# A two-block transformer step: the attention output product in two halves, and the output written before a branch

## The reference

```python
mod = jnp.einsum('bd,de->be', jax.nn.silu(c), w_ada[l]) + b_ada[l]
sh1, sc1, g1, sh2, sc2, g2 = [m[:, None, :] for m in jnp.split(mod, 6, axis=-1)]
h = _rms(x, norm1_g[l]) * (1.0 + sc1) + sh1
c_q, c_kv, k_pe, dq, dk, dv = jnp.split(h @ w_in[l], IN_SPLITS, axis=-1)
o_mla = _mla(c_q, c_kv, k_pe, ...)       # 8 heads x 64; q from w_uq, k and v from w_ukv
o_diff = _diff_attn(dq, dk, dv, ...)     # 4 heads x 128, each head's output under _rms
x = x + g1 * (jnp.concatenate([o_mla, o_diff], axis=-1) @ w_o[l])
h2 = _rms(x, norm2_g[l]) * (1.0 + sc2) + sh2
x = x + g2 * _hmoe(h2, ...)              # 2 of 16 experts per token, D_EXPERT = 512
```

## Time and profile before

| | us |
|---|---|
| median of 3 runs | 2050.57 (2049.27 to 2053.07) |
| profiled execution | 2052.58 |
| its span, first to last instruction | 2050.7 |
| PE busy | 1840.4 (90%) |
| DVE, ACT, POOL busy | 620.0, 486.7, 351.6 |
| mean granted TensorE clock | 0.936 |

### The profile page before, as it was taken

How to read it: one execution, slowest core, us unless ns; L and a number is a source line. 1 busy time by engine, 2 the same in 40 slices (tenths; PEclk the granted TensorE clock), 3 DMA queues, 4 the chain that set the end, 5 groups by cost and what they waited for, 6 DMA issues and landing times.

```text
span 2050.7 us, 29034 instructions
## 1 busy us (share of the span) xinstructions
PE 1840.4 (90%) x12173; PEld 1078.1 (53%) x12173; DVE 620.0 (30%) x1265; ACT 486.7 (24%) x830; POOL 351.6 (17%) x306
## 2 busy tenths in 40 slices
PE   8999999989957699999999999999995896599996
PEld 7977999757935333323332333233322786454442
DVE  6777554346444500100000000010004585501102
ACT  5844443324402110001000010000002553321120
POOL 3000000000000399999920000000001000000000
PEclk9998999988978699999999999999997988789998
DMA  6446664446522899999999999999995440569994
GB/s 191 152 137 205 207 206 172 159 154 207 185 82 82 300 408 404 417 415 411 409 409 417 411 411 404 419 410 411 402 421 157 129 144 1 205 266 419 420 419 199
DMA packets 185008, 583.04 MB, mean 284 GB/s; under 512 B 11162, under 2 KB 77355, under 8 KB 158241
## 3 DMA queue, kind: packets, MB, share of 16 engines
q1 hardware_dynamic: 182256, 575.09, 73.1%
q0 software_dynamic: 2608, 5.97, 1.1%
HBM read 579.96 MB, written 1.05 MB: 283 GB/s over the span
## 4 chain that ended last, share of the span: by engine, by line
PE 70%; DMA 13%; DVE 9%; ACT 4%; issue 2%; SPq 2%; DVEq 0%; ACTq 0%
PE ps L1702 16%; PE ps L440 9%; PE ps L441 8%; PE ps L442 8%; DMA ring<-in_moe_w_out 8%; PE ps L2137 6%; PE ps L1707 5%; PE ps L1738 4%; DMA ring<-in_moe_w_in 3%; PE ps L2161 3%; SPq L1550 1%; DVE wlo L473 1%; PE ps L1743 1%; PE ps L575 1%; PE ps L2122 1%
## 5 line engine op out<-in xcount | busy, mean ns | idle before, releaser
L1702 PE MATMUL ps<-ring,xg 128*64 128x512 f32 x1624 | 411.7, 602 | 13.1 <-ACT sgm L1812 5.8
L473 DVE TENSOR_TENSOR wlo<-raw,whi 128x2048 fp32r<-128x2048 f32 (+6 forms) x97 | 213.8, 2208 | 227.8 <-ACT whi L465 227.5
L1702 PEld LDWEIGHTS ps<-ring,xg 128*64 128x64 f32 x1624 | 121.8, 137 | 220.0 <-issue 208.6
L465 ACT ACTIVATE whi<-raw 128x2048 fp32r<-128x2048 f32 (+6 forms) x97 | 178.7, 1845 | 230.5 <-PE ps L442 89.3
L440 PE MATMUL ps<-xh,whi 128*128 128x272 f32 (+1 forms) x712 | 212.7, 299 | 4.1 <-DVE xl L540 3.8
L1738 PE MATMUL ps<-ring,ahm 128*64 128x512 f32 x824 | 204.5, 597 | 11.7 <-DMA ring<-in_moe_w_out 10.9
L442 PE MATMUL ps<-xh,wlo 128*128 128x272 f32 (+1 forms) x712 | 210.0, 295 | 0.0
L441 PE MATMUL ps<-xl,whi 128*128 128x272 f32 (+1 forms) x712 | 209.7, 295 | 0.0
L2070 POOL TENSOR_SCALAR lnt<-lnt,h 128x384 f32<-128x384 f32 x120 | 188.6, 1572 | 12.2
L1876 DVE TENSOR_TENSOR sgm<-sgm,ps 128x512 f32<-128x512 f32 x28 | 18.2, 685 | 512.2 <-PE ps L1707 512.2
L704 POOL DMA_DIRECT2D lnt<-in_ln_gain x4 | 2.2, 560 | 858.1 <-issue 525.6
(11 more groups left out here) (567 smaller groups left out, 2471.4 us busy)
## 6 DMA issues: line engine op xcount, KB each, us to landing
ring<-in_moe_w_in SPq DMA_DIRECT2D x203, 1024.0 KB, 17.9
ring<-in_moe_w_out SPq DMA_DIRECT2D x103, 1024.0 KB, 19.9
ring<-in_w_gate SPq DMA_DIRECT2D x29, 1024.0 KB, 13.2
raw<-in_ffn_w_in SPq DMA_DIRECT2D x28, 1024.0 KB
ring<-in_w_down SPq DMA_DIRECT2D x26, 1024.0 KB, 12.6
raw<-in_w_ada SPq DMA_DIRECT2D x24, 1024.0 KB
more<-in_moe_w_in SPq DMA_DIRECT2D x21, 1024.0 KB, 18.1
ring<-in_w_up SPq DMA_DIRECT2D x20, 1024.0 KB, 11.5
```

The costliest lines, as they stand in the source:

```text
L465: e.activation(whi[0:rows, s % NSPL, 0:n], raw[0:rows, i % NRAW, 0:n], ACT.Copy).then_inc(S.hi.s, S.hi.up((s,)))
L473: e.tensor_tensor(wlo[0:rows, s % NSPL, 0:n], raw[0:rows, i % NRAW, 0:n], whi[0:rows, s % NSPL, 0:n].bitcast(F32), ALU.subtract).then_inc( ...
L1702: e.matmul(ps_[b][64 * v:64 * v + 64, :], a[:, kk_, 64 * v:64 * v + 64], both[v][:, k, 512 * b:512 * b + 512], start=kk_ == 0, stop=kk_ == 7)
```

## The change

- Start: ScalarE's split of w_in's first chunk goes behind the two squares.
- `dve_neighbours_end` goes from behind the angles to right behind the cq turn.
- VectorE's low part of w_in's last chunk goes ahead of the k products.
- x6 is cut in two. Its first four column blocks (the MLA heads) are turned between `values 2` and `probs 3`; `wo` chunks 0 and 1 are multiplied right behind `values 3`, under the norm of the differential heads. The last four (x6b) follow when `od` is ready, then chunks 2 and 3, first all of group 0, then all of group 1 (`pe_last_two`, which is used with XTILES elsewhere).
- Gate, sum, mean square and root are done group by group; ScalarE scales both groups; the transposes of group 0 for x7 (the first four) come ahead of group 1's.
- The end: VectorE multiplies by g2 out of PSUM and adds to h within the first round; SyncE writes the output ahead of its branch. Where the further rounds run, they add to h and write it again.

The diff, cut to what the text speaks of (signal names, the labels and the unchanged half of the first norm are left out):

```diff
@@ -620,7 +620,7 @@
             bank.give((key, 2), (dve, key, "sum", 2))
-        for t, n, cc in XTILES:
+        for t, n, cc in tiles:
             for m in range(4):
@@ -2286,13 +2286,10 @@
             for q in range(2):
-                o = w["y"][:, t, 512 * q:512 * q + 512]
-                p = bk(key, "Y", t, q)[:, :]
-                if r == 0:
-                    ins = e.tensor_copy(o, p)
-                else:
-                    ins = e.tensor_tensor(o, o, p, ALU.add)
-                ins.then_inc(C.dve.s, C.dve.up((key, "out")))
+                a = slice(512 * q, 512 * q + 512)
+                e.tensor_tensor(w["y"][:, t, a], bk(key, "Y", t, q)[:, :], g2t[:, a], ALU.mult).then_inc(C.dve.s, C.dve.up((key, "out")))
+            e.wait_ge(C.dve.s, C.dve.n)
+            e.tensor_tensor(h[:, t, :], h[:, t, :], w["y"][:, t, :], ALU.add).then_inc(C.dve.s, C.dve.up((key, "result", t)))
@@ -2302,6 +2299,7 @@
                 load_ring(e, C, SLOTS, False)
+                sp_out_again(e)
             for r, key in enumerate(ROUNDS2):
@@ -2312,6 +2310,8 @@
                         e.wait_ge(C.dve.s, C.dve.n)
+                    else:
+                        e.wait_ge(landed["out"].s, landed["out"].at("all"))
                     dve_pairs(e, C, key, w2, r + 1)
@@ -2356,22 +2356,45 @@
-    def act_mean_sq(e, key, full):
+    def act_mean_sq(e, s):
         for t in range(2):
-            e.wait_ge(dve.s, dve.at(full, t))
+            e.wait_ge(dve.s, dve.at("ln3", t))
             e.activation(hn[:, t, :], h[:, t, :], ACT.Square, scale=1.0 / 32, accum_out=rs[:, 0, t:t + 1]).then_inc(
-                act.s, act.up((key, "sum")))
-        if key == "rms2":
-            act_spread(e, "g2", g2t)
-        e.wait_ge(dve.s, dve.at(key, "root"))
-        e.activation(hn[:, 0, :], h[:, 0, :], ACT.Copy, scale=rs[:, 1, 0:1]).then_inc(act.s, act.up((key, "hn")))
-    def dve_mean_sq(e, key):
-        e.wait_ge(act.s, act.at(key, "sum"))
+                act.s, act.up(("rms1", "sum")))
+        split_hi(e, M, s)
+        e.wait_ge(dve.s, dve.at("rms1", "root"))
+        e.activation(hn[:, 0, :], h[:, 0, :], ACT.Copy, scale=rs[:, 1, 0:1]).then_inc(act.s, act.up(("rms1", "hn")))
...
+    def act_gated_norm(e):
+        for t in range(2):
+            e.wait_ge(dve.s, dve.at("x1", t))
+            e.activation(hn[:, t, :], h[:, t, :], ACT.Square, scale=1.0 / 32, accum_out=rs[:, 0, t:t + 1]).then_inc(
+                act.s, act.up(("rms2", "sum", t)))
+            if t:
+                act_spread(e, "g2", g2t)
+            e.wait_ge(dve.s, dve.at("rms2", "root", t))
+            e.activation(hn[:, t, :], h[:, t, :], ACT.Copy, scale=rs[:, 1, t:t + 1]).then_inc(act.s, act.up(("rms2", "hn", t)))
+    def dve_gated_norm(e):
+        e.wait_ge(act.s, act.at("spread", "g1", 1))
+        for t in range(2):
+            e.wait_ge(pe.s, pe.at("wo", "tile", t))
+            for q in range(2):
+                a = slice(512 * q, 512 * q + 512)
+                e.tensor_tensor(pj[:, t, a], bank("wo", t, q)[:, :], g1t[:, a], ALU.mult).then_inc(dve.s, dve.up(("wo", "sum", t)))
+            e.wait_ge(dve.s, dve.n)
+            e.tensor_tensor(h[:, t, :], h[:, t, :], pj[:, t, 0:1024], ALU.add).then_inc(dve.s, dve.up(("x1", t)))
+            e.wait_ge(act.s, act.at("rms2", "sum", t))
+            e.tensor_scalar(rs[:, 0, t:t + 1], rs[:, 0, t:t + 1], RMS_EPS, None, ALU.add).then_inc(dve.s, dve.up())
+            dve_rsqrt(e, rs[:, 1, t:t + 1], rs[:, 0, t:t + 1], rtmp[:, t:t + 1], ("rms2", "root", t))
@@ -2612,12 +2635,12 @@
         pe_values(e, 2)
+        e.wait_ge(dve.s, dve.at("o1"))
+        pe_turn(e, "x6", src_n, QTILES, 4)
         pe_probs(e, 3)
         pe_values(e, 3)
-        e.wait_ge(dve.s, dve.at("od"))
-        pe_turn(e, "x6", src_n, QTILES, 8)
         acc = {(t, q): bank.take(e, "wo", t, q) for t, _, _ in QTILES for q in range(2)}
-        for j in range(4):
+        for j in range(2):
             wh, wl = (w.rearrange("p (i n) -> p i n", i=2) for w in weights(e, M, ("wo", j)))
@@ -2625,14 +2648,30 @@
                         ins = mm3(e, acc[t, q][:, :], xh[:, k, cc:cc + n], xl[:, k, cc:cc + n],
-                                  wh[:, i, 512 * q:512 * q + 512], wl[:, i, 512 * q:512 * q + 512], k == 0, k == 7)
-            ins.then_inc(pe.s, pe.up(("wo", j), used(M, ("wo", j))))
-        for t, q in acc:
-            bank.give(("wo", t, q), (dve, "gated", t, q))
+                                  wh[:, i, 512 * q:512 * q + 512], wl[:, i, 512 * q:512 * q + 512], k == 0, False)
+            ins.then_inc(pe.s, pe.up(used(M, ("wo", j))))
+        e.wait_ge(dve.s, dve.at("od"))
+        pe_turn(e, "x6b", lambda t, k: src_n(t, 4 + k), QTILES, 4)
+        e.wait_ge(dve.s, dve.at("x6b", "lo", 3))
+        pe_last_two(e, "wo", acc, None, [("wo", 2), ("wo", 3)],
+                    lambda m, cc, n: (xh[:, 4 + m, cc:cc + n], xl[:, 4 + m, cc:cc + n]), [], QTILES)
         pe_spread(e, "g2", pool)
-        e.wait_ge(act.s, act.at("rms2", "hn"))
-        e.wait_ge(dve.s, dve.at("rms2", "hn"))
-        pe_turn(e, "x7", src_n, QTILES, 8)
+        p = {}
+        def turn(k, t):
+            if t == 0:
+                p[k] = bank.take(e, "x7", k)
+            return e.transpose(p[k][:, 128 * t:128 * t + 128], src_n(t, k), idn)
+        e.wait_ge(act.s, act.at("rms2", "hn", 0))
+        for k in range(4):
+            turn(k, 0)
+        e.wait_ge(act.s, act.at("rms2", "hn", 1))
+        for k in range(8):
+            if k >= 4:
+                turn(k, 0)
+            turn(k, 1).then_inc(pe.s, pe.up(("x7", "T", k)))
+            bank.give(("x7", k), (dve, "x7", "lo", k))
         pe.label(("end_mid",))
@@ -2641,8 +2680,7 @@
         act_spread(e, "g1", g1t)
-        split_hi(e, M, s)
-        act_mean_sq(e, "rms1", "ln3")
+        act_mean_sq(e, s)
         split_hi(e, M, s + 1)
@@ -2707,14 +2745,14 @@
         act_probs(e, 2)
+        act_turn(e, "x6", QTILES, 4, xh)
         act_probs(e, 3)
         e.wait_ge(dve.s, dve.at("o2"))
         e.activation(od2, od, ACT.Square).then_inc(act.s, act.up(("osq",)))
-        act_turn(e, "x6", QTILES, 8, xh, gain_o)
-        for j in range(4):
-            split_hi(e, M, s)
-            s += 1
-        act_mean_sq(e, "rms2", "x1")
+        split_hi(e, M, s)
+        s += 1
+        act_turn(e, "x6b", QTILES, 4, xh[:, 4:8], gain_o)
+        act_gated_norm(e)
         act_turn(e, "x7", QTILES, 8, xh, gain_x3, shift_x3, tmpT)
@@ -2825,13 +2863,13 @@
         dve_turn(e, "cq", QTILES, 5, cq[:, 0], cq[:, 1], gain_cq)
+        dve_neighbours_end(e)
         split_lo(e, M, s)
         s += 1
         e.wait_ge(act.s, act.at("lat"))
         e.tensor_scalar(rs[:, 0, 0:4], r4[:, :], RMS_EPS, None, ALU.add).then_inc(dve.s, dve.up())
         dve_rsqrt(e, r4[:, :], rs[:, 0, 0:4], rtmp[:, 0:4], ("r4",))
         dve_angles(e)
-        dve_neighbours_end(e)
         for j in range(3):
@@ -2853,15 +2891,16 @@
         dve_head_rms(e, "ksq", 96, 64, pe2[:, :], rk16)
+        split_lo(e, M, s)
+        s += 1
         e.wait_ge(dve.s, dve.n)
         e.tensor_tensor(k5[:, :, :, 0:64], k5[:, :, :, 0:64], rk16[:, :, :].unsqueeze(3).to_broadcast([128, 2, 8, 64]), ALU.mult).then_inc(
             dve.s, dve.up())
         for t in range(2):
             e.tensor_tensor(k4[t][:, :, 64:96], kpe[:, t, :].unsqueeze(1).to_broadcast([128, 8, 32]),
                             rk16[:, t, :].unsqueeze(2).to_broadcast([128, 8, 32]), ALU.mult).then_inc(dve.s, dve.up(("kk",)))
-        for _ in range(2):
-            split_lo(e, M, s)
-            s += 1
+        split_lo(e, M, s)
+        s += 1
         for i in range(2):
@@ -2885,8 +2924,10 @@
         dve_values(e, 1)
+        dve.label(("o1",))
         dve_probs(e, 2)
         dve_values(e, 2)
+        dve_turn(e, "x6", QTILES, 4, xh, xl)
         dve_probs(e, 3)
@@ -2899,25 +2940,15 @@
         e.tensor_tensor(od, od, r1.unsqueeze(3).to_broadcast([128, 2, 4, 128]), ALU.mult).then_inc(dve.s, dve.up(("od",)))
-        dve_turn(e, "x6", QTILES, 8, xh, xl, gain_o)
-        for j in range(4):
-            split_lo(e, M, s)
-            s += 1
-        e.wait_ge(pe.s, pe.at("wo", 3))
-        e.wait_ge(act.s, act.at("spread", "g1", 1))
-        for t in range(2):
-            for q in range(2):
-                a = slice(512 * q, 512 * q + 512)
-                e.tensor_tensor(pj[:, t, a], bank("wo", t, q)[:, :], g1t[:, a], ALU.mult).then_inc(dve.s, dve.up(("gated", t, q)))
-                e.wait_ge(dve.s, dve.n)
-                e.tensor_tensor(h[:, t, a], h[:, t, a], pj[:, t, a], ALU.add).then_inc(dve.s, dve.up(("x1", t)))
-        dve_mean_sq(e, "rms2")
+        split_lo(e, M, s)
+        s += 1
+        dve_turn(e, "x6b", QTILES, 4, xh[:, 4:8], xl[:, 4:8], gain_o)
+        dve_gated_norm(e)
         dve_turn(e, "x7", QTILES, 8, xh, xl, gain_x3, shift_x3, tmpT)
         dve.label(("end_mid",))
         return s
-    y2 = w2["y"]
```

(33 more changed lines are left out.)

4 lines of the change are left out of this document (2 added, 2 removed).

## The result

The changed kernel is faster. In a first timing its median was 2024.9 us against 2049.9 us (ratio 0.9872, 95% interval 0.9843 to 0.9900), in a second, on another occasion, 2029.0 against 2051.3 (0.9887, 0.9867 to 0.9906). That is 26 and 23 us, where the forecast had 22.2. The first median lies inside the range, 0.9 us above its low end of 2024; the ratio times the median of before, 2049.9, gives 2023.7, just under it. The times alone do not refute 22.2, which lies inside both intervals (20.5 to 32.2 us and 19.3 to 27.3). The profiles, cut into stages, do: the four gains are there nearly as forecast, and the gain as a whole is about 4 us larger.

The account below looks back on a forecast made before the run. TensorE was taken to bound the expert pairs, with the attention part a serial stretch whose waits also lower the clock. A 2.8 + B 5.8 + C 10.4 + D 3.2 = 22.2 us off 2050.6: 2028.4, range 2024 to 2038.

Parts of the forecast that it names:

- A: Start of the stage: squares ahead of w_in's first split, sums ready sooner; gain 2.8 us (1.5 to 2.9).
- B: w_uq to first scores: no vp wait, ukv sooner, w_in's last chunk at full clock; gain 5.8 us (4.3 to 7.5).
- x6 in front: Between the heads: x6's first transposes, copies and subtractions ahead of values 3 cost 1.7 us.
- C: Output product: first half under the differential heads' norm, end by groups; gain 10.4 us (8 to 10.8), net of 1.7.
- D: Kernel's end: g2 multiplied out of PSUM, output DMA ahead of SyncE's branch; gain 3.2 us (2.4 to 5).
- Rival 1: Clock falls once more, ahead of values 3 or w_in's last chunk: costs 1.7 in C, 1.5 in B; 2031.6 us; 24%.
- Rivals 2 and 5: 2: A and B end at something unmoved, 2037 us; 5: w_o's first half not under the norm, 2036; together 15%.
- The prediction's row: Head transposes: clock rose to 1.00 at 1679.5 and stayed to 1686.9, read as transposes keeping it up.
- whatever the attention part saves arrives at the end as it is: Expert pairs: eight rounds of 28.2 us at clock 1.00 stay unchanged, if the weights keep pace.
- rival 3: Expert pairs: gains ahead of them are given back, DMA share being 1.01; D alone remains, 2047 us; 5%.

Follow-up runs that it names:

- only_wo: Kernel before with only x6 in two halves, half of w_o's product during the heads' norm and the end by token groups: ratio 0.9932.
- wo_output: Kernel before with the w_o halves, the end by token groups and the output ahead of SyncE's branch, without the first two gains: ratio 0.9925.
- fill: Changed kernel with 36 and 10 unused matmuls in TensorE's waits for the router's masks and for sel: ratio 0.9870.

## Why the prediction was right and where it fell short

Means over the profiles with and without each part, in us:

| stage | without | with | gain | forecast |
|---|---|---|---|---|
| gc to scores 0 (A, B) | 105.6 (7 profiles) | 97.0 (8) | 8.6 | 8.6 |
| scores 0 to norm (x6 in front) | 46.0 (7) | 46.8 (9) | -0.8 | -1.7 |
| norm to sel (C) | 64.7 (7) | 52.2 (10) | 12.5 | 12.1 |
| sel to last sg | 217.9 (7) | 217.0 (4) | 0.9 | 0 |
| last sg to y | 25.5 (5) | 23.4 (4) | 2.1 | 0 |
| y to end (D) | 14.7 (8) | 11.8 (9) | 2.9 | 3.2 |
| sum | | | 26.2 | 22.2 |

- **A was right**: 2.8 alone.
- **B was right in its parts**, within 0.5: the 4 us ahead of w_ukv, the fallen clock there, the shrunken wait and the last chunk at full clock. Rival 1's clock fall ahead of the last chunk did not come in any profile. Behind the chunk lies a wait that the prediction doesn't name, the 1.8 us for `qk`, and in five of the nine profiles with B the clock fell there.
- **C was right**: 12.5 for 12.1. For the 1.7 us of x6 between the heads I have 0.8 out of two groups that each spread over 4 to 6 us; this size stays open. The wait ahead of values 3 was 2.5 us for the forecast's 3.0, and the clock stayed up in all profiles of the changed kernel. In `only_wo` and `wo_output` the same 2.5 us wait was followed at once by 3.4 us at 0.50, into the w_o product. So rival 1's fall in C was near, and its way of telling safe waits from others, by their length alone (2.3 against 2.9 us), is not borne out. Rivals 2 and 5 are out.
- The Trainium skill, TensorE: Matmul & The Clock Gate, "Part 4: PE-mode transpose", has transposes not counting as busy. x6's eight don't decide on it: they took 1.0 us, from 1701.0, when the clock rose behind 3.4 us of products. The prediction's row does not either as it was read, since 5.2 of its 7.4 us are score products. But the same trace of before disagrees with the page, in two places. At the stage's start TensorE sat idle and then ran x5's 16 transposes and nothing else; at the head transposes it had run w_in's last chunk. Windows over the idle time, x5 up to the rise, and what follows; then over the chunk, the first 4 us of head transposes, and the last of them:

```profile
1571.50:1584.30 12.80, 0.00 (x0) 0.50 1.03 294
1584.40:1587.20 2.80, 2.80 (x13) 0.50 0.02 7
1587.40:1594.00 6.60, 3.94 (x22) 1.00 0.49 156
...
1666.10:1675.20 9.10, 9.10 (x45) 0.50 0.62 230
1675.30:1679.30 4.00, 4.00 (x20) 0.50 0.54 156
1679.50:1680.80 1.30, 1.30 (x14) 1.00 0.65 271
```

  The clock rose behind 2.9 us of x5's transposes, with 12.9 us of idle ahead of them. At the heads 9 us of 128x160 products left it low, and it rose 4.1 us into the transposes.
- **D was right**: 2.9 for 3.2, the branch 3.6 for 3.4. Alone it gave 2.2: y to the end took 12.5 us, 0.8 more than in the changed kernel, with VectorE's four steps as long as there; the 0.8 lies between the last sum and the end, and its cause is open.
- **The step that failed is "whatever the attention part saves arrives at the end as it is"**, with the pairs entered as zero: 3.0 us came there. The earlier trace rows shows one round in the middle, at 1.00, and I read all eight from it. Five of the seven distances from one `sg` to the next are 28.2 us; the first is 20.5 and the last 23.7, so eight rounds of 28.2 was a misreading too. Their first 16 us ran at the low level and their end had a fall of 3.4 us, which windows over the trace of before show. The change made the rise come 1.8 us sooner after sel (14.8 for 16.6 in the means), which gave 0.9, and moved the wait past the fall, which gave 2.1. Together 3.0 of the 4.0 us that the sum lacks; the rest is C and the x6 term, less D. The 2.1 came by a narrow margin that nobody aimed at: 209.66 in one profile, where 209.60 fell. That direction, gains in the pairs, was in no rival: rival 3 had them only give back, and they didn't.
- **The low end of the range was too high** for that reason, and because a term of chance is missing: 10 us between profiles ahead of `gc`, 6 us in the attention.

Open: why the rise comes sooner after sel with A, B and C together than with C alone (15.2 and 16.0 against 14.7 to 15.0). The distances are close, and two profiles are few. Open too is what sets the distances at which the clock changes.

## What to carry to other kernels

Read the granted clock at the edges of a dense stretch, not only in its middle: behind a serial part the first products can run at half speed, and a forecast that enters the stretch as unchanged has assumed the clock unchanged. A wait of TensorE costs its length and what runs slow behind it, if the clock falls, and closing some of the waits ahead of dense work can be worth nothing: `fill` left two open, of 1.95 and 1.59 us, and gained nothing; closing the first of these brought 4.0 us, closing the other 1.6 more. Where a sum of stages is compared with a measured total, profile both kernels twice: the first pair differed by 33.9 us, of which about 8 were chance.
